# Forgetting-attention heads 2 to 11: gate and query projections as seven block products, with the weight sums on VectorE, the input normed ahead, and outputs parked in DRAM

## The reference

```python
q, r = jnp.split(rmsnorm(h, norm_g) @ w_in, 2, axis=-1)      # w_in: 1024 x 4096
q = q.reshape(B, L, 16, 128).transpose(0, 2, 1, 3) * 128 ** -0.5
s = jnp.einsum('bhqd,bhkd->bhqk', q, k) + cum[..., :, None] - cum[..., None, :]
p = jax.nn.softmax(jnp.where(causal, s, NEG_INF), axis=-1)
o = jnp.einsum('bhqk,bhkd->bhqd', p, v)
return h + (o * jax.nn.silu(r)) @ w_out
```

## Time and profile before

| | |
|---|---|
| median of three runs | 1021.08 us (1020.34 to 1021.25) |
| span of the profiled execution | 1019.0 us |
| TensorE busy (the page's PE) | 1011.9 us, 99% |
| VectorE busy (DVE) | 633.8 us, 62% |
| ScalarE busy (ACT) | 509.8 us, 50% |
| GpSimd busy (POOL) | 39.8 us, 4% |
| DMA, HBM read and written | 91.53 MB and 4.23 MB |

### The profile page before, as it was taken

The page is one execution under the profiler, slowest core; times in us unless marked ns, Lnnn a source line. Parts: engine busy times, 40 slices in busy tenths (PEclk is TensorE's granted clock), DMA queues, the critical chain, the costliest instruction groups (busy, mean ns, idle before and its releaser), DMA issues.

```text
span 1019.0 us, 17745 instructions
## 1 busy us (share of the span) xinstructions
PE 1011.9 (99%) x7267; PEld 924.8 (91%) x7267; DVE 633.8 (62%) x1050; ACT 509.8 (50%) x858; POOL 39.8 (4%) x69
## 2 busy tenths in 40 slices
PE   9999999999999999999999999999999999999998
PEld 8999999999999999997888888888888888888887
DVE  6875666577467785448666547765566647686332
ACT  6754654554474553236455526554445526574332
POOL 0000000000000000000110001100010001110000
PEclk9999999999999999999999999999999999999999
DMA  8221221221122114331434224344344223333412
GB/s 288 75 72 63 82 85 45 81 84 64 63 84 84 64 44 146 111 111 56 139 135 96 90 83 111 89 95 105 78 124 109 90 83 110 89 91 108 148 53 83
DMA packets 36625, 97.10 MB, mean 95 GB/s; under 512 B 4144, under 2 KB 12208, under 8 KB 36544
## 3 DMA queue, kind: packets, MB, share of 16 engines
q1 hardware_dynamic: 35824, 95.29, 31.1%
q10 hardware_dynamic: 720, 0.68, 0.2%
HBM read 91.53 MB, written 4.23 MB: 94 GB/s over the span
## 4 chain that ended last, share of the span: by engine, by line
PE 98%; DMA 1%; ACT 0%; DVE 0%; issue 0%; SPq 0%; DVEq 0%; ACTq 0%
PE psum L1499 73%; PE psum L1792 9%; PE psum L1848 3%; PE psum L1624 2%; PE psum L1829 2%; PE psum L1572 1%; PE psum L1816 1%; PE psum L1818 1%; PE psum L1817 1%; PE psum L1620 1%; PE psum L1593 1%; PE psum L1758 1%; PE psum L1552 1%; DMA hT<-xT 1%; PE psum L1834 1%; PE psum L1618 0%
## 5 line engine op out<-in xcount | busy, mean ns | idle before, releaser
L893 DVE TENSOR_TENSOR w_lo<-raw,w_hi 128x1024 fp32r<-128x1024 f32 x143 | 172.4, 1217 | 57.1 <-ACT w_hi L482 56.7
L482 ACT ACTIVATE w_hi<-raw 128x1024 fp32r<-128x1024 f32 x143 | 149.6, 1052 | 58.9 <-PE psum L1792 39.6
L1499 PE MATMUL psum<-xh,w_hi 128*128 128x264 f32 x768 | 159.1, 288 | 1.0 <-DVE w_lo L900 0.6
L1499 PE MATMUL psum<-xl,w_hi 128*128 128x264 f32 x768 | 155.9, 285 | 0.0
L1499 PE MATMUL psum<-xh,w_lo 128*128 128x264 f32 x768 | 155.3, 283 | 0.0
L1499 PEld LDWEIGHTS psum<-xh,w_hi 128*128 128x128 f32 x768 | 118.5, 189 | 2.5 <-DVE xl L915 1.9
L1499 PEld LDWEIGHTS psum<-xl,w_hi 128*128 128x128 f32 x768 | 119.5, 188 | 0.0
L1499 PEld LDWEIGHTS psum<-xh,w_lo 128*128 128x128 f32 x768 | 119.0, 188 | 0.0
L1499 PE MATMUL psum<-y_lo,w_hi 128*128 128x264 f32 (+2 forms) x400 | 104.8, 314 | 0.0
L1499 PE MATMUL psum<-x2h,w_hi 128*128 128x512 f32 x256 | 103.5, 404 | 0.0
L1499 PE MATMUL psum<-x2h,w_lo 128*128 128x512 f32 x256 | 101.4, 396 | 0.0
(11 more groups left out here) (283 smaller groups left out, 2057.7 us busy)
## 6 DMA issues: line engine op xcount, KB each, us to landing
raw<-w_all SPq DMA_DIRECT2D x143, 512.0 KB, 3.3
sub<-sums SPq DMA_DIRECT2D x16, 264.0 KB, 7.4
sub<-sums SPq DMA_DIRECT2D x16, 200.0 KB, 6.3
sub<-sums SPq DMA_DIRECT2D x16, 136.0 KB, 4.9
hT<-xT SPq DMA_DIRECT2D x8, 264.0 KB, 6.0
h_keep<-hT SPq DMA_DIRECT2D x8, 256.0 KB, 4.1
hT<-h_keep SPq DMA_DIRECT2D x8, 256.0 KB, 5.1
sub<-sums SPq DMA_DIRECT2D x16, 72.0 KB, 3.4
```

The lines of the kernel that those rows point to most:

```text
L482: nc.scalar.activation(w_hi[:, n % HI_RING, :], raw[:, n % LO_RING, :], ACT.Copy).then_inc(hi_made, 1)
L893: nc.vector.tensor_tensor(w_lo[:, n % LO_RING, :], raw[:, n % LO_RING, :], w_hi[:, n % HI_RING, :].bitcast(F32), ALU.subtract).then_inc(lo ...
L1499: i = nc.tensor.matmul(o, w[a][:, k % KT, :], x[b][:, k, c0:c1], start=k == first and a == b == 0, stop=k == last and a == 1)
```

## The change

**Seven products in place of eight.** For the heads of `strassen(h)` (2 to 11) strips `r<h>` and `q<h>` are made together. The two weights are the blocks' columns, the two halves of the 1024 input rows the inner index, and the two halves of the 512 tokens the outer one: a 2 x 2 by 2 x 2 block product, done by seven products with sums of blocks (Winograd's form of Strassen). A product is four k tiles by three passes by 256 columns, 12 matmuls, in place of two strips of 24 matmuls of 512 columns.

**Sums.** The sums of the token blocks (`token_sums`, four of 128 x 1024) are made once, in head 0, and split by ScalarE and VectorE (`t_hi`, `t_lo`). The sums of the weight blocks (`weight_sums`, four of 128 x 512 on VectorE) are made for each head; they fill `s1_raw`, half of the `q` chunk and a new ring slot `e<h>`, which is split like a chunk but isn't loaded. The sums of the products (`first_sums`, `second_sums`, `last_sum_of`) are VectorE's as well, one of 512 and five of 256 columns.

**Norm.** The input is multiplied by `rstd` once (`norm`, two of 128 x 2048) and then split (`x2h` by two copies on ScalarE, `norm_lo` on VectorE), so `fox_gate` and `fox_query` lose their multiply, and ScalarE reads those strips from PSUM. The eight STTs that made `x2l` in the loop over `W0` to `W7` are gone.

**Outputs.** The outputs of heads 0 to 10 stay in `sq` and are written to DRAM (`y_keep`, 256 KB each), since `y` now holds the sums; they are read back from head 12 on.

**Order between the layers.** `LOWF` and `m0` come before the last two k tiles of `k0`, and `q0` comes after `u0`.

```diff
+S0, NS = 2, 12
+def strassen(h):
+    return S0 <= h < NS
...
+PRODUCTS = (1, 5, 2, 6, 7, 4, 3)
...
+            def weight_sums(h):
+                i = h - S0
+                r, q, e = (CHUNK[f"{x}{h}"] for x in "rqe")
...
+                nc.vector.tensor_tensor(s1_raw[:], w21, w22, ALU.add).then_inc(sum_made, 1)
+                dve.wait_ge(sum_made, 4 * i + 1)
+                nc.vector.tensor_tensor(w21, w21, w11, ALU.add).then_inc(sum_made, 1)
+                wait_chunk_used(dve, e - LO_RING)
+                nc.vector.tensor_tensor(s2, s1_raw[:], w11, ALU.add).then_inc(sum_made, 1)
+                dve.wait_ge(sum_made, 4 * i + 3)
+                nc.vector.tensor_tensor(s4, s2, w12, ALU.add).then_inc(sum_made, 1)
...
+            def product(o, w, k0, x):
+                for k in range(KT // 2):
+                    for a, b in PARTS:
+                        i = nc.tensor.matmul(o, w[a][:, k0 + k, :], x[b][:, k, :], start=k == a == b == 0, stop=k == KT // 2 - 1 and a == 1)
+                i.then_inc(prod_done, 1)
...
+            def middle_products(h):
+                product(bank(7, HS, SEQ), weights(f"e{h}"), 0, mt2)
+                w = weights(f"q{h}")
+                pe.wait_ge(copied, h - S0 + 1)
+                product(bank(0, HS, SEQ), w, 0, t3)
+                pe.wait_ge(kf_made, h + 1)
+                product(bank(2, 0, HS), w, 4, t4)
...
             for h in range(H):
+                if strassen(h):
+                    pe.wait_ge(out_made, output(h, "21"))
+                    wait_slot(pe, f"k{h + 1}")
+                    if n:
+                        key_part(h + 1, range(0, n))
+                    fox_scores(h)
+                    key_part(h + 1, range(n, KT)).then_inc(job_done, 1)
...
+                if h + 1 < H and strassen(h + 1):
+                    first_products(h + 1)
+                    transpose_probs(h)
+                    middle_products(h + 1)
+                    pe.wait_ge(out_made, output(h + 1, "11"))
+                    fox_attend(h)
+                    if last:
+                        end_values(fox_group(h))
+                    last_product(h + 1)
+                    if last:
+                        fox_values(fox_group(h))
+                    continue
```

```diff
@@ scalar, before head 0: the copies of x2h stand between the forget gate's steps @@
-            ahead("k0")
+            end_groups_out(0)
+            split_to("u02")
+            act.wait_ge(x2_normed, 1)
+            nc.scalar.activation(x2h[:, 0:4, :], x2n[:, 0:4, :], ACT.Copy).then_inc(x2h_made, 1)
             act.wait_ge(f_logit, 1)
@@ scalar, head 0, after probs_hi @@
+                if h == 0:
+                    for n in range(4):
+                        act.wait_ge(t_made, 4)
+                        nc.scalar.activation(t_hi[:, n], t_raw[:, n], ACT.Copy).then_inc(thi_made, 1)
@@ vector, end of a FoX step @@
                 fox_out(h)
+                if strassen(h + 2):
+                    weight_sums(h + 2)
```

More of the change, by code:

```diff
@@ L95, in gla_jobs, with fox_group, fox_chunks @@
                      f"A{h}1", f"X{h}2", f"V{h}3", f"A{h}2", f"X{h}3", f"R{h}3", f"A{h}3"] + ([f"G{h + 1}0"] if h + 1 < GLA_HEADS else []))
+def strassen(h):
+    return S0 <= h < NS
+def fox_group(h):
+    return (h + 1) // VH if h + 1 < FOX_HEADS and (h + 1) % VH == 0 else None
 def fox_step(h):
[L100 to L108, removed]
+    group = fox_group(h)
+    jobs = [] if strassen(h) else [f"r{h}"]
+    if h + 1 == FOX_HEADS:
+        return jobs + [f"a{h}"]
+    jobs += [f"k{h + 1}"]
+    ends = [] if group is None else [f"m{group}"]
+    jobs += [f"a{h}"] + ends if strassen(h + 1) else ends + [f"q{h + 1}", f"a{h}"]
+    return jobs + ([] if group is None else [f"u{group}"])
+def fox_chunks(h):
+    group = fox_group(h)
+    chunks = [] if strassen(h) else [f"r{h}"]
+    if h + 1 < FOX_HEADS:
+        chunks += [f"k{h + 1}"]
+        chunks += [f"r{h + 1}", f"q{h + 1}", f"e{h + 1}"] if strassen(h + 1) else [f"q{h + 1}"]
+    return chunks + ([] if group is None else [f"u{group}{c}" for c in range(VH)])
 JOBS = (["LOW"] + [j for h in range(GLA_HEADS) for j in gla_jobs(h)] + [f"W{d}" for d in range(KT)]
-        + ["k0", "LOWF", "m0", "q0", "u0"] + [j for h in range(FOX_HEADS) for j in fox_step(h)] + [f"w{d}" for d in range(KT)])
+        + ["LOWF", "m0", "k0", "u0", "q0"] + [j for h in range(FOX_HEADS) for j in fox_step(h)] + [f"w{d}" for d in range(KT)])
 JOB = {j: n for n, j in enumerate(JOBS)}
@@ L229, in program @@
                     cum_t = sb("cum_t", [P, NBLK, FOX_HEADS], F32, three)
+                    with ExitStack() as four:
+                        ends = sb("ends", [P, 2, AF_ALL], F32, four)
                     a_hi = sb("a_hi", [P, AF_ALL], F32R, three)
@@ L283, in end_groups @@
         def end_groups(g):
-            i = 8 if g < NBLK - 1 else 12
-            return [y[0:META, i + n, 0:VH * P] for n in range(4)]
+            if g in (0, NBLK - 1):
+                return [y[0:META, (12 if g else 8) + n, 0:VH * P] for n in range(4)]
+            return [ends[0:META, n // 2, n % 2 * VH * P:(n % 2 + 1) * VH * P] for n in range(4)]
         def joined(b):
@@ L467, in _, with mask_sums @@
             pool.wait_ge(cst_loaded, 16)
-            for h in range(FOX_HEADS):
+            def mask_sums(h):
                 for b in range(NBLK):
@@ L472, in _ @@
                     nc.gpsimd.tensor_tensor(diag, diag, above, ALU.add).then_inc(sub_made, 1)
+            mask_sums(0)
+            for h in range(FOX_HEADS):
+                if h + 1 < FOX_HEADS:
+                    mask_sums(h + 1)
         @block.scalar
@@ L1975 @@
     chunks = []
-    for name in CHUNKS:
+    for name in LOADED:
         n = int("".join(x for x in name if x.isdigit()))
```

555 lines of the change are left out of this document (405 added, 150 removed).

## The result

| | before | after |
|---|---|---|
| median | 1020.73 us (four runs, 1020.34 to 1021.25) | 1029.01 us (four runs, 1027.92 to 1029.53) |
| ratio of the medians | | 1.0081, 95% interval 1.0066 to 1.0095 |
| profiled execution, its own time | not given | 1027.92 us, span 1026.1 us |

A forecast was written before the change was run, and what follows sets the result against it. TensorE, busy 1011.9 of 1019.0 us, was taken as the bound. -13.1 + 7.5 + 5.8 + 0.6 + 2.8 + 3.9 + 2.0 = +9.5 gave a span of 1028.5, plus 2.1 to the median: 1030.6 us, range 1022 to 1037.

The forecast's parts named there:

- columns saved: TensorE, ten seven-product heads: seven products take 9.89 us in place of 11.20, saving 1.31 a head, 13.1 in all.
- heads 4 and 8: Start of these heads, behind `u1` and `u2`: TensorE waits 1.95 us for chunk `e` twice, 3.9 in all.
- `u02`: Between the layers: TensorE waits 1.7 us more at the third chunk of `u0`, for its split on VectorE.
- `e2`: Behind head 1's maxima: four more VectorE splits of 1024 elements leave a wait of 0.6 us at this split.
- the seven heads: Heads 2, 3, 5, 6, 7, 9, 10: TensorE waits 0.4 us in each for chunk `e`, 2.8 in all.
- clock: Behind both early waits TensorE's clock falls to half rate: 2.0 us for both, between 0 and 5.5.
- Place 1: Between the layers: TensorE waits 5.9 us for `f_sum`, then 1.7 for `u02`; taken as 7.5, between 5 and 9.
- Place 2: Head 0 to head 1: token sums delay the scores of head 1, TensorE waits 5.8 us; bounds 4.5 to 6.5.
- Place 3: Each seven-product head: TensorE waits for chunk `e`, 2.8 us in seven heads, 3.9 in heads 4 and 8; bounds 0, 11.
- The rival that VectorE becomes the bound: Seven-product heads: VectorE's instructions 5% longer, 0.6 us a head, each wait following on the last: 1035 us; chance 0.17.
- The second rival: Seven-product heads: Place 3 has no waits, while the early waits stand: 1023.9 us; chance 0.16.
- The first rival: Whole kernel: VectorE and ScalarE keep up, nothing waits, only the columns saved count: 1008 us; chance 0.12.

The follow-up runs named there:

- all_moved: Changed kernel with token sums, forget gate, group-end sums and splits, `e` splits, `m0` adds and first keys reordered, no instruction added or removed: 1011.1 us, ratio 0.9907.
- sums_in_idle: Changed kernel with token sums, their copies and rests, and the split of `k1` moved to other places in head 0: 1022.1 us, ratio 1.0013.
- one_more_on_vector: Changed kernel plus one unread VectorE minimum over 528 columns ahead of the split of `e` in each seven-product head: 1036.8 us, ratio 1.0158.
- gates_first: Changed kernel with the forget logits' adds and the forget gate's steps ahead of the input's norm between the layers: 1023.9 us, ratio 1.0032.
- fill_the_waits: Changed kernel plus unread matmuls, 50 ahead of `u0` and 42 ahead of the scores of head 1: 1028.0 us, ratio 1.0070.

## Why the prediction was right, term by term

The forecast of 1030.6 was 1.6 above the median, and the side is right: what VectorE had to do ahead of TensorE's next work cost more than the columns saved. Of the six waits that it named three came, in their places (`f_sum`, the scores of head 1, heads 4 and 8), and three didn't (`u02`, `e2`, the seven heads); one came that it hadn't named (`k1`).

That the number came so close is in part luck. By the terms the waits were forecast at 20.6 and found at 14.5, 6.1 too much; against that stood 1.6 too much of columns saved, 1.5 too little of clock, and 0.7 not foreseen, so that the span grew by 7.1 for 9.5. Another 0.8 came back in the step from span to median: 2.1 by the kernel before, 2.9 here, where the trace is of the fastest execution.

The stretch of heads 1 to 12 in the changed kernel, less what all_moved takes for it, splits as 5.13 = 2.57 of waits + 1.76 of clock + 0.80 that isn't taken apart (shorter waits and slower first matmuls).

| term | predicted | found | where |
|---|---|---|---|
| columns saved | -13.1 | -11.5 | 21.60 for 22.76 a head |
| wait for `f_sum` | 5.9 | 6.00 | at 472.60 |
| wait for the split of `u02` | 1.7 | 0 | 1.17 with full clock |
| scores of head 1 | 5.8 | 5.11 | at 533.93 |
| split of `e2` | 0.6 | 0 | 0.38 with full clock |
| seven heads at 0.4 | 2.8 | 0 | 0.13 early |
| heads 4 and 8 | 3.9 | 2.57 | at 644.24 and 756.59 |
| clock | 2.0 | 3.46 | 1.70 and 1.76 |
| split of `k1` | none | 0.78 | at 511.97 |
| rest | none | +0.7 | +0.45, -0.55, +0.80 |

**Place 1**: the wait for `f_sum` was read right, to 0.1 us, from rows of before. The chain on VectorE is the cause: with it reordered the wait is 0.91. That most of the clock's return would lie over the wait for `u02` was right as well; I then charged 1.7 for the one and left 2.0 for the clock, together 3.7, and found 3.46.

**Place 2** was right in mechanism and 0.7 too long. The run that moved only this work took the wait away. What I missed is `k1`: in the new order of chunks its split stands on VectorE behind the maxima of head 0, with two more behind it, and its strip was 0.78 early. The prediction followed only the splits of `e` and of `u0`.

**Place 3** was right in kind; the size was off. I laid VectorE's chain to the split of `e` at 15.4 against TensorE's 15.0. From the end of the values, at 650.68, it took 15.04 against 15.17. Some 0.5 us in 15 made 2.8 us of forecast into none, since it lay on the edge. Heads 4 and 8 were 0.7 each too long in the same way. Adding 0.6 a head brought the waits back in nine heads. The rival that VectorE becomes the bound was priced at 0.6 a head and 1035; this is that case, and it took 1036.8. The second rival, place 3 free, is true of all heads but 4 and 8.

**The columns** were off by 1.6, against the waits; only the seven heads (2.8) and `u02` (1.7) were further off. I took 0.1177 a step of 256 columns from the last strip; the products run at 0.1194 (35 steps in 4.18 us in all_moved), 0.14 a head, 1.4 of the 1.6 that are missing. The seven products stand in three groups, with a first matmul that is 0.1 us slower behind each other kind of work (0.21 from 650.68 in the changed kernel), as the strips did. The forecast's sum of TensorE's own work in a head, 21.3, is short too: 22.76 less its 1.31 is 21.45.

**The clock** lost 3.5 on TensorE. The Trainium skill, TensorE: Matmul & The Clock Gate, "HAM oscillation — how this bites in real kernels", says that a long enough wait for data puts the array back to half rate, so that the next group starts cold. Both long waits agree. The forecast took from the end of the old trace that the clock falls 3.4 us after the last work, and reasoned that both early waits are longer. That was no fixed measure: windows of 0.2 us put the fall 2.7 us after the last work in the first wait and 1.9 in the second, and 4.5 in the first wait of sums_in_idle, where the clock came back later too and more of `u0` was slow. Nor must a wait be that long: behind 1.54 (sums_in_idle), 1.90 and 1.95 (one_more_on_vector) the clock fell as well, at 751.5, 763.6 and 647.6, that is 0.5 to 0.8 us after TensorE had started again. Behind 1.28 and 1.29, 1.31 and 1.46 (gates_first) and 1.45 (fill_the_waits) it stayed full.

The first rival, that the other engines keep up, is what all_moved shows: 1008 was its forecast, and with 1.8 of waits left and 1.6 less saved it came to 1011.1. The change as such pays; its order between the layers and in head 0 cost more than it paid. That the parked outputs cost nothing agrees with the trace, in which no wait of TensorE over 0.2 us is released by a DMA; it wasn't tried by itself, and nor were the norm ahead of the split and the `x2l` left out.

## What to carry to other kernels

Ask of an engine with idle time not how much it has, but how early it is at each point where the bound engine asks for something; the timelines of the old kernel give that to some tenths, and 0.1 us early in every head is the same as full. New work of a few microseconds that has no hurry goes into a stretch where its engine waits for someone, ahead of nothing that the bound engine is about to ask for. Put right what is late at once and in all places: each wait taken away shows the one that it covered.

## What wasn't expected of the hardware

A fall of the clock can pay for itself in part: slow TensorE gave VectorE 1.7 us, and a full clock turned up a wait of 1.17 that hadn't been there. The clock fell behind waits of 1.54 to 1.95 us and stayed full behind those of up to 1.46, and behind one and the same wait of 6.00 it cost 1.7 us in one trace and 2.5 in another. The kernel with these falls (sums_in_idle) spread from 1020.5 to 1023.6 in ten executions, all_moved, which has none, over 0.7 us in four. That the falls make the spread is likely, but not shown: only one execution of each was traced, and the kernel before, at full clock too, spread over 1.9 us in sixteen.
